# Two chained blocks on one core: the opening operands in three groups, the second expert block requested in the routing phase, and down weights as one run per partition

## What is computed

```python
silu_c = jax.nn.silu(c)
sh1, sc1, gt1, sh2, sc2, gt2 = jnp.split((silu_c @ ada_w[layer] + ada_b[layer])[:, None, :], 6, axis=-1)
...
hid = jnp.sin(freq * (feats @ w1 + b1))
hid = jnp.sin(freq * (hid @ w2 + b2))
filt = hid @ w3
filt = filt * jnp.exp(-t[:, None] * deltas[None, :])
filt = filt / jnp.sum(jnp.abs(filt), axis=0, keepdims=True)
...
def expert_block(args):          # once per block of rows of one expert
    xblk, e = args
    return (jax.nn.silu(xblk @ w1[e]) * (xblk @ w3[e])) @ w2[e]
```

## Time and profile before

| | us |
|---|---|
| median of 3 runs | 4396.33 (4392.52 to 4397.52) |
| the profiled execution | 4396.28 |
| its span, first to last instruction | 4394.5 |
| mean granted TensorE clock | 0.958 |

### The profile page before, as it was taken

One profiled execution on the slowest core, in us unless ns is written; L12 is line 12 of the kernel. 1 busy time (PEld: TensorE's weight loads), 2 busy tenths in 40 slices (PEclk: granted clock), 3 DMA queues, 4 the chain that ended last, 5 costly groups with the idle time before them and its releaser, 6 DMA issues. The chain is left out here.

```text
span 4394.5 us, 95415 instructions
## 1 busy us (share of the span) xinstructions
PE 3982.7 (91%) x41485; PEld 2613.4 (59%) x41485; DVE 1482.2 (34%) x2542; ACT 1014.7 (23%) x2416; POOL 605.7 (14%) x732
## 2 busy tenths in 40 slices
PE   7798999998999969999978999989999989997995
PEld 2343446885444458888854444469888944445774
DVE  2555412133121320000042666655566532222003
ACT  2200110032010112222243442034444311112333
POOL 1030000001100000000010001334454311000112
PEclk8899999999999979999989999989999999997997
DMA  6362302003112079999971001100000031124998
GB/s 214 117 200 81 129 24 72 29 10 66 38 37 93 34 286 390 391 396 398 396 250 28 10 2 43 43 2 4 4 3 4 4 97 43 58 84 183 392 388 316
DMA packets 233424, 588.67 MB, mean 134 GB/s; under 512 B 36456, under 2 KB 140807, under 8 KB 213224
## 3 DMA queue, kind: packets, MB, share of 16 engines
q1 hardware_dynamic: 192447, 462.92, 28.9%
q0 software_dynamic: 19120, 73.68, 4.9%
q10 hardware_dynamic: 21626, 48.70, 3.2%
HBM read 514.20 MB, written 71.05 MB: 133 GB/s over the span
## 5 line engine op out<-in xcount | busy, mean ns | idle before, releaser
L1650 PE MATMUL experts_bank<-experts_uT,ex_wu 128*64 128x96 f32 x9216 | 391.5, 247 | 27.0 <-PE experts_bank L1636 21.3
L1650 PEld LDWEIGHTS experts_bank<-experts_uT,ex_wu 128*64 128x64 f32 x9216 | 385.1, 138 | 43.7 <-issue 43.7
L1723 DVE TENSOR_TENSOR experts_hT<-experts_si,experts_bank 128x384 f32<-128x384 f32 (+1 forms) x68 | 31.3, 460 | 723.1 <-PE experts_bank L1650 723.1
L192 PE MATMUL vgproj_bank<-vg_w,mix_hT 128*128 128x256 f32 x1024 | 225.7, 383 | 11.1 <-DVEq L201 7.7
L192 PEld LDWEIGHTS vgproj_bank<-vg_w,mix_hT 128*128 128x128 f32 x1024 | 195.7, 192 | 41.5 <-DVEq L201 8.5
L1650 PE MATMUL experts_bank<-experts_uT,b2z_hT 128*64 128x96 f32 x4096 | 177.7, 248 | 25.3 <-DMA b2z_hT<-in_w 12.7
L1650 PEld LDWEIGHTS experts_bank<-experts_uT,b2z_hT 128*64 128x64 f32 x4096 | 172.2, 138 | 40.0 <-issue 40.0
L1636 PE MATMUL experts_bank<-mixed_T,experts_hT 128*32 128x256 f32 (+1 forms) x2592 | 193.9, 451 | 0.0
L2247 POOL TENSOR_TENSOR b2z_hT<-b2z_hT,rwkv_level 128x256 f32<-128x256 f32 x192 | 153.8, 833 | 159.3 <-DVE b2z_hT L2600 159.2
L2616 DVE TENSOR_TENSOR rc_xy<-rc_xy,rc_bank 128x256 f32<-128x256 f32 x288 | 120.6, 420 | 122.3 <-PE rc_bank L2261 116.4
L1636 PEld LDWEIGHTS experts_bank<-mixed_T,experts_hT 128*32 128x32 f32 x2592 | 110.4, 110 | 69.6
(11 more groups left out here) (576 smaller groups left out, 7195.4 us busy)
## 6 DMA issues: line engine op xcount, KB each, us to landing
ex_wu<-in_expert_w SPq DMA_DIRECT2D x72, 2048.0 KB
mixed_T<-in_expert_w SPq DMA_DIRECT2D x36, 2048.0 KB, 23.0
b2z_hT<-in_w SPq DMA_DIRECT2D x64, 1024.0 KB
b2z_Z<-in_w SPq DMA_DIRECT2D x32, 1024.0 KB, 12.4
keep_rows<-mix_hyT ACTq DMA_DIRECT2D x27, 768.0 KB
keep_rows<-experts_yo ACTq DMA_DIRECT2D x68, 288.0 KB
mix_hT<-in_ada_w POOLq DMA_DIRECT2D x8, 2048.0 KB, 9.9
merge_w<-in_w_in SPq DMA_DIRECT2D x32, 512.0 KB, 6.1
```

Source lines behind the costliest of these rows:

```text
L192: last = pe.matmul(bk[t][:, 0:width], xT[:, k, t * P:(t + 1) * P], wt[:, s, k, :], start=(k == 0), stop=(k == KT - 1))
L1650: last = pe.matmul(bk[2 + j][c:c + 64, h * BT:(h + 1) * BT], wu[:, s, j, k, h * P + c:h * P + c + 64], uT[:, s, k, :], start=(k == 0), sto ...
```

## The change

Three edits. (1) The opening: ACT's nine operands are split into `fed` (features, first layer), `layered` (the three vectors and the second layer) and `spread` (third layer, `negt`, `delta`), and each user waits for its own group. The first 16 of the 23 vectors stay on SP's queue, the other 7 are requested by ACT between `layered` and `spread`. POOL waits for `layered` before its first request of `ada_w`. (2) The routing phase requests the weights of block zero and of block one, and the loop of the expert phase starts with block two; its last load outside the loop is gone. (3) `w2` is laid out by `experts_to_runs` too, so that partition p holds the hidden rows 4p to 4p+3 (2p and 2p+1 in the second mixture). For the hidden values to come out in that order, the up products take as stationary operand every fourth (every second) column of `wu`, which is a step of 16 (8) bytes.

```diff
--- before.py
+++ after.py
@@ -154,10 +154,6 @@
 def rows_to_tiles(ap):
 
     return ap.rearrange("l (k p) n -> p (l k) n", p=P)
-
-
-def experts_to_tiles(ap):
-    return ap.rearrange("l e (k p) n -> p (l e) k n", p=P)
 
 
 def experts_to_runs(ap):
@@ -612,20 +608,25 @@
         wfull = m.sems(*[f"wfull{n}" for n in range(RING)])
         loaded, zeroed, turned, cols_ok, silu_ok, ada_mm, ada_out, ada_cols = m.sems(
             "loaded", "zeroed", "turned", "cols_ok", "silu_ok", "ada_mm", "ada_out", "ada_cols")
-        come, browed, lin, chain, sine, mm, decs, fls, abss, sums = m.sems(
-            "come", "browed", "lin", "chain", "sine", "mm", "decs", "fls", "abss", "sums")
+        fed, layered, spread, browed, lin, chain, sine, mm, decs, fls, abss, sums = m.sems(
+            "fed", "layered", "spread", "browed", "lin", "chain", "sine", "mm", "decs", "fls", "abss", "sums")
         vectors = [v for v in VECS if v]
         ada_w = rows_to_tiles(I["ada_w"])
         b = m.block()
+        SPLIT = 16
+
+        def row_of(name, n):
+
+            g, r = divmod(PLACES[name][0], P)
+            return rows[r:r + n, g, :], flat(I[name]).rearrange("(n p) -> n p", p=P)
 
         @b.sync
         def _(sp):
             sp.dma_start(K.ident[:, :], I["k_eye"]).then_inc(loaded, 16)
             sp.dma_start(adasum[:, :], I["k_adasum"]).then_inc(loaded, 16)
             sp.wait_ge(zeroed, 1)
-            for name, n in vectors:
-                g, r = divmod(PLACES[name][0], P)
-                sp.dma_start(rows[r:r + n, g, :], flat(I[name]).rearrange("(n p) -> n p", p=P)).then_inc(loaded, 16)
+            for name, n in vectors[:SPLIT]:
+                sp.dma_start(*row_of(name, n)).then_inc(loaded, 16)
 
         @b.gpsimd
         def _(gp):
@@ -636,6 +637,7 @@
             gp.memset(one2[:, :], 0.0).then_inc(zeroed, 1)
             gp.wait_ge(zeroed, 5)
             gp.memset(one2[:, 0:2], 1.0).then_inc(zeroed, 1)
+            gp.wait_ge(layered, 64)
             for n in range(ADA):
                 if n >= RING:
                     gp.wait_ge(ada_mm, ada_item(n - RING) + 1)
@@ -684,13 +686,14 @@
                 if t >= 1:
                     norm_sum(t - 1)
 
-            pe.wait_ge(come, 16 * 9)
+            pe.wait_ge(fed, 32)
             for x in range(2):
                 pe.matmul(fm[x][0:64, :], w1[:, :], feats[:, x * HALF:(x + 1) * HALF], start=True, stop=True).then_inc(lin, 1)
             pe.wait_ge(loaded, 16 * (2 + len(vectors)))
             for g in range(VGROUPS):
                 pe.transpose(cb[:, g * P:(g + 1) * P], rows[:, g, :], K.ident[:, :]).then_inc(turned, 1)
             pe.wait_ge(sine, 1)
+            pe.wait_ge(layered, 64)
             for x in range(2):
                 pe.matmul(fm[x][0:64, :], w2[:, :], hid[:, x * HALF:(x + 1) * HALF], start=True, stop=True).then_inc(lin, 1)
             pe.wait_ge(silu_ok, 2)
@@ -701,6 +704,7 @@
                 ada_rows(n)
                 ada_turn(n - 1)
             pe.wait_ge(sine, 2)
+            pe.wait_ge(spread, 48)
             for t in range(NT):
                 filt(t)
                 if t in (1, 3, 4, 6):
@@ -715,11 +719,16 @@
 
         @b.scalar
         def _(act):
-            loads = [(feats[:, :], I["k_feats"]), (w1[:, :], I["hy_ffn_w1"][0]), (vecs[:, 0:1], I["hy_ffn_b1"].rearrange("a p -> p a")),
-                     (vecs[:, 1:2], I["hy_ffn_freq"].rearrange("a p -> p a")), (vecs[:, 2:3], I["hy_ffn_b2"].rearrange("a p -> p a")),
-                     (w2[:, :], I["hy_ffn_w2"][0]), (w3[:, :], I["hy_ffn_w3"][0]), (negt[:, :], I["k_negt"]), (delta[:, :], I["k_delta"])]
-            for dst, src in loads:
-                act.dma_start(dst, src).then_inc(come, 16)
+            for to, what in ((feats[:, :], I["k_feats"]), (w1[:, :], I["hy_ffn_w1"][0])):
+                act.dma_start(to, what).then_inc(fed, 16)
+            for to, what in ((vecs[:, 0:1], I["hy_ffn_b1"].rearrange("a p -> p a")), (vecs[:, 1:2], I["hy_ffn_freq"].rearrange("a p -> p a")),
+                             (vecs[:, 2:3], I["hy_ffn_b2"].rearrange("a p -> p a")), (w2[:, :], I["hy_ffn_w2"][0])):
+                act.dma_start(to, what).then_inc(layered, 16)
+            act.wait_ge(zeroed, 1)
+            for name, n in vectors[SPLIT:]:
+                act.dma_start(*row_of(name, n)).then_inc(loaded, 16)
+            for to, what in ((w3[:, :], I["hy_ffn_w3"][0]), (negt[:, :], I["k_negt"]), (delta[:, :], I["k_delta"])):
+                act.dma_start(to, what).then_inc(spread, 16)
             act.dma_start(brow[:, :], I["ada_b"]).then_inc(browed, 16)
 
             def ada_evac(n):
@@ -750,6 +759,7 @@
             act.wait_ge(chain, 12)
             act.activation(hid[:, :], arg[:, :], ACT.Sin).then_inc(sine, 1)
             ada_evac(3)
+            act.wait_ge(spread, 48)
             for t in range(NT):
                 if t >= 2:
                     act.wait_ge(fls, 2 * (t - 1))
@@ -767,7 +777,7 @@
         @b.vector
         def _(dve):
             then = Chain(dve, chain)
-            dve.wait_ge(come, 16 * 9)
+            dve.wait_ge(layered, 64)
             for n in range(2):
                 dve.wait_ge(lin, 2 * n + 2)
                 if n:
@@ -1346,10 +1356,11 @@
                 sp.wait_ge(yok, t + 1)
                 sp.dma_start(y_dram[tok(t), :], ys[:, t % SLOTS, :]).then_inc(ysaved[t % SLOTS], 16)
             sp.wait_ge(chosen, 1)
-            e = sp.value_load(T.be[0:1, 0:1], min_val=0, max_val=NE - 1)
-            for j, wj in enumerate((w1, w3)):
-                sp.dma_start(T.wu[:, 0, j, :, :], wj[:, bass.ds(e, 1), :, :].rearrange("p a k n -> p (a k) n")).then_inc(T.wufull[0], 16)
-            sp.dma_start(T.wd[:, 0, :, :], w2[:, bass.ds(e, 1), :, :].rearrange("p a k n -> p (a k) n")).then_inc(T.wdfull[0], 16)
+            for n in range(2):
+                e = sp.value_load(T.be[0:1, n:n + 1], min_val=0, max_val=NE - 1)
+                for j, wj in enumerate((w1, w3)):
+                    sp.dma_start(T.wu[:, n, j, :, :], wj[:, bass.ds(e, 1), :, :].rearrange("p a k n -> p (a k) n")).then_inc(T.wufull[n], 16)
+                sp.dma_start(T.wd[:, n, :, :], w2[:, bass.ds(e, 1), :, :].rearrange("p a k n -> p (a k) n")).then_inc(T.wdfull[n], 16)
 
         @b.gpsimd
         def _(gp):
@@ -1599,11 +1610,9 @@
 
             n1 = sp.value_load(T.nb[0:1, 1:2], min_val=1, max_val=MAXB // 2 - 1)
             with sp.Fori(0, n1) as i:
-                for s in (1, 0):
-                    e = sp.value_load(T.be[0:1, bass.ds(i * 2 + (2 - s), 1)], min_val=0, max_val=NE - 1)
-                    load(s, e, i * 2 + (3 - s))
-            e = sp.value_load(T.be[0:1, bass.ds(n1 * 2 + 1, 1)], min_val=0, max_val=NE - 1)
-            load(1, e, n1 * 2 + 2)
+                for s in range(2):
+                    e = sp.value_load(T.be[0:1, bass.ds(i * 2 + (2 + s), 1)], min_val=0, max_val=NE - 1)
+                    load(s, e, i * 2 + (3 + s))
             for dst, src, sem in ahead:
                 sp.dma_start(dst, src).then_inc(sem, 16)
 
@@ -1647,7 +1656,7 @@
                         for h in range(HT):
                             for k in range(KT):
                                 for c in (0, 64):
-                                    last = pe.matmul(bk[2 + j][c:c + 64, h * BT:(h + 1) * BT], wu[:, s, j, k, h * P + c:h * P + c + 64],
+                                    last = pe.matmul(bk[2 + j][c:c + 64, h * BT:(h + 1) * BT], wu[:, s, j, k, :].rearrange("p (q h) -> p h q", h=HT)[:, h, c:c + 64],
                                                      uT[:, s, k, :], start=(k == 0), stop=(k == KT - 1))
                         last.then_inc(up, 1)
                     pe.wait_ge(xfull[1 - s], i * 16 + (16 + 16 * s))
@@ -3216,7 +3225,7 @@
 
 
     rgw, rgb, rew, reb, w1, w3, w2 = names
-    ws = (experts_to_runs(I[w1]), experts_to_runs(I[w3]), experts_to_tiles(I[w2]))
+    ws = tuple(experts_to_runs(I[n]) for n in (w1, w3, w2))
     with Mem(nc, f"ex{tag}") as mx:
         T.wu = mx.sb("wu", [P, 2, 2, KT, hidden]) if wu is None else wu.rearrange("p k (s n) -> p (k s) n", n=hidden).rearrange("p (s j k) n -> p s j k n", s=2, j=2)
         T.be = mx.sb("be", [1, MAXB], I32)
```

## The result

The changed kernel takes 4556.54 us (median of 4 runs, 4551.66 to 4559.55) where the kernel before takes 4396.93 (4392.52 to 4399.69): a ratio of 1.0366, 95% interval 1.0353 to 1.0379. Forecast were 4384.7 us, in a range of 4371 to 4400. The profiled execution took 4557.07 us (span 4555.3), 160.8 more than the span before.

A forecast was written before the change was run, and what follows sets the result against it. TensorE, busy 91% of the span, was taken as the bound, so savings count only where it waits. 4396.3 - 13.1 (opening) + 2.5 + 2.0 (entries) - 3.0 (stage-two waits) = 4384.7 us, range 4371 to 4400.

The forecast's parts named there:

- rival 2: Up products, first stage alone: strided halves take turns at the load at the 16-byte step; +110 us, 4495 us, chance 0.07.
- The opening: Start of the program: the first product no longer waits for all nine operands; 13.1 us gained, range -15 to -6.
- the 1.5 us forecast for the fourth item: Opening, fourth `ada_w` load: lands at about 32.5 us, wanted at 31, so TensorE waits 1.5 rather than 1.2 us.
- the -15 of the range: Start of the program: the largest gain allowed for the opening, in a range of -15 to -6 us, clock uncertain.
- The entries: Start of both expert stages: block zero's gather competes with more queued weights; +2.5 us in the first, +2.0 in the second.
- +9: Both stage entries together: upper bound, if the gather takes 9.3 us in stage two and 2 us more in stage one.
- The waits at the end of stage two: Up products of stage two: a lead of a whole block removes the excess wait for weights; -3.0 us, other bound 0.
- w2 by runs, the SP loop: Expert stages: longer w2 runs help only where DMA is awaited, and the reordered loop issues the same loads; 0 us.
- The columns: Up products: the strided rate is the rate of plain fp32 loads, so strided columns cost 0; bounds 0 and 24 ns a pair.
- The rule quoted beside it: Strided loads: the skill's 16-byte cachelines need two hits for full rate, so 8-byte steps are free and 16-byte ones not.
- Rival 1: Up products, both stages: strided halves take turns at the load, 24 ns a pair; +159 us, 4544 us, chance 0.10.
- 0 to 24 ns: Up products: bounds on the extra load time of a pair of strided halves, the upper if they take turns.

The follow-up runs named there:

- the kernel without part 3: The changed kernel with w2 by tiles of 4 KB rows and contiguous columns, keeping the new opening and block one's early weight requests: 4389.71 us, ratio 0.9988.
- e11: Opening in three groups only, with w1 and w3 laid out by pairs of rows, so transposes load columns 8 bytes apart: 4395.80 us, ratio 0.9995.
- part 1 alone: The kernel before with only the opening in three groups of operands: 4384.48 us, ratio 0.9971.
- e6: The kernel before, stage one's column groups read at 4, 8, 12 and 16 bytes, transposes contiguous; only durations count: 81, 82.5, 87, 119 ns a pair.
- part 2 alone: The kernel before with only block one's weights requested in the routing phase and the reordered SP loop: 4402.47 us, ratio 1.0017.
- part 3 alone: The kernel before with only w2 by runs and the strided columns: 4565.75 us, ratio 1.0391.

## Why the columns cost

**An 8-byte step in both stages.** The changed kernel with w2 in two runs of two rows for each partition of stage one, so that the columns of an up product lie 8 bytes apart:

```
-    wu[:, s, j, k, :].rearrange("p (q h) -> p h q", h=HT)[:, h, c:c + 64]
+    wu[:, s, j, k, :].rearrange("p (a q h) -> p a h q", a=HT // 2, h=2)[:, h // 2, h % 2, c:c + 64]
-    w2: "l e (p k) n -> p (l e) k n"
+    w2: "l e (a p h) n -> p (l e) a (h n)", h=2
```

> The changed kernel with another order of the hidden units in stage one: a partition gets w2 as two runs of two rows (8 KB each), so the stationary operand of the up products is read with 8 bytes between columns in both stages; stage two is as in the changed kernel. Theory: only steps of 16 bytes and more load slower; the up products of stage one are back at 10.8 us a block (85 ns a pair of halves), and the time is that of the kernel without part 3, 4390 us (ratio 0.9988). Rival: any step costs once 36 blocks of four column groups are read, and stage two is spared only because it waits for its weights anyway: between 4390 and 4556.

Measured: 4389.52, 0.9989 (0.9980 to 0.9997), what parts 1 and 2 alone give:

```profile
L1659 PE MATMUL experts_bank<-experts_uT,ex_wu 128*64 128x96 f32 x9216 | 390.2, 247 | 26.2 <-PE experts_bank L1645 22.0 <-ACT experts_uT L1687 2.9 <-issue 1.3
```

Of the two steps only that of 16 bytes costs. This is rival 2 of the prediction.

**Steps of 4 to 16 bytes side by side.** This run and the three like it below are one execution each; only durations inside it are read. In stage one each of the four column groups has its own step and its own line:

```
+    wu[:, s, j, k, 0:64]     wu[:, s, j, k, 448:512]      (L1656, L1657)
+    wu[:, s, j, k, 0:128:2]  wu[:, s, j, k, 384:512:2]    (L1659, L1660)
+    wu[:, s, j, k, 0:192:3]  wu[:, s, j, k, 320:512:3]    (L1662, L1663)
+    wu[:, s, j, k, 0:256:4]  wu[:, s, j, k, 256:512:4]    (L1665, L1666)
     transposes: xg[:, slot, k * P:(k + 1) * P]
```

> The kernel before; in stage one the four column groups of an up product are read with 4, 8, 12 and 16 bytes between columns, each on a source line of its own, and the transposes of the gathered rows read contiguous columns instead of 32 bytes apart. It computes with the wrong columns, so only durations count. Theory (a load runs at full rate only when two of its columns lie in one 16-byte piece of memory; this is what the Trainium skill says in SBUF - State Buffer, in its note on cachelines): a pair of halves takes 85 ns at 4 and 8 bytes; at 12 bytes half of the columns have a neighbour in their piece, so 0.75 of 122 = 92 ns; at 16 bytes 122 ns. The eight transposes, 0.96 us before, fall to 0.6 or less. Rivals: the cost grows with the distance crossed (85, 97, 110, 122); or it belongs to the pair of halves alone and a single load has one rate whatever its step: then the transposes stay at 0.96.

The first load of each group of 16 pairs, from the timeline of PEld:

```profile
1910.93 0.13 PEld L1656 LDWEIGHTS experts_bank<-experts_uT,ex_wu 128*64 128x64 f32 x1 [0.86 <-issue]
...
1912.22 0.14 PEld L1659 LDWEIGHTS experts_bank<-experts_uT,ex_wu 128*64 128x64 f32 x1
...
1913.54 0.16 PEld L1662 LDWEIGHTS experts_bank<-experts_uT,ex_wu 128*64 128x64 f32 x1
...
1914.93 0.20 PEld L1665 LDWEIGHTS experts_bank<-experts_uT,ex_wu 128*64 128x64 f32 x1
...
1916.83 0.15 PEld L1656 LDWEIGHTS experts_bank<-experts_uT,ex_wu 128*64 128x64 f32 x1
```

From start to start, over 16: 81, 82.5, 87 and 119 ns a pair for 4, 8, 12 and 16 bytes, where 85, 85, 92 and 122 were expected; the rival of a cost that grows with the distance (97 at 8 bytes) is out. The transposes, now contiguous, take 0.70 us of loads for eight, not the 0.6 or less expected, but less than the 0.96 of before, and 62.9 us in all instead of 79.8:

```profile
1904.35 0.70 PEld L1631 LDWEIGHTS experts_bank<-all_ident,ex_xg 96*128 96x128 f32 x8
...
L1631 PEld LDWEIGHTS experts_bank<-all_ident,ex_xg 96*128 96x128 f32 x560 | 49.9, 143 | 24.7 <-issue 17.5
```

So a strided load is slower there too (204 ns against 143, the same instruction at another step), which the prediction had explained away.

**Larger steps, and one half strided alone.** Column groups: first half 4 bytes and second 16 (L1656, L1657), then both 32, both 20, both 24.

> The kernel before; in stage one the column groups are read with these bytes between columns, each on a line of its own: first half 4 and second half 16; both 32; both 20; both 24. It computes with the wrong columns, so only durations count. Theory (full rate needs two columns in one 16-byte piece, and the loads of the two halves follow one another): 32, 20 and 24 bytes all cost what 16 did, 122 ns a pair; the mixed pair takes 61 ns for the strided half and at most 32 for the contiguous one, 85 to 93. Rival 1: halves conflict only when both are strided: 85 mixed. Rival 2: the cost grows with distance or comes from powers of two: 32 bytes far above 122, or 20 and 24 below it.

```profile
1898.31 0.13 PEld L1656 LDWEIGHTS experts_bank<-experts_uT,ex_wu 128*64 128x64 f32 x1 [1.38 <-issue]
1898.32 0.19 PEld L1657 LDWEIGHTS experts_bank<-experts_uT,ex_wu 128*64 128x64 f32 x1
...
1900.22 0.22 PEld L1660 LDWEIGHTS experts_bank<-experts_uT,ex_wu 128*64 128x64 f32 x1
...
1902.18 0.21 PEld L1663 LDWEIGHTS experts_bank<-experts_uT,ex_wu 128*64 128x64 f32 x1
...
1904.01 0.21 PEld L1666 LDWEIGHTS experts_bank<-experts_uT,ex_wu 128*64 128x64 f32 x1
...
1905.87 0.22 PEld L1657 LDWEIGHTS experts_bank<-experts_uT,ex_wu 128*64 128x64 f32 x1
```

The second halves (L1657, L1660, L1663, L1666) advance every 119 ns at 16 bytes, 122 at 32, 114 at 20 and 116 at 24: from 16 bytes on, the distance changes little, and powers of two nothing. But the mixed pair was expected at 85 to 93 ns, and it runs at 119, no faster than with both halves strided. That is no sum of two loads. The theory that the halves' loads follow one another fell here, and so did rival 1, by which halves conflict only when both are strided.

**Loads of one half, and of all columns.** Stage one again: one half behind the other with 4 bytes (L1656, L1658), the same with 16 (L1660, L1662), 128 columns with 4 (L1664), 128 with 16 (L1666).

> The kernel before; in stage one the column groups are read so: loads of one half only, one behind the other, 4 bytes between columns; the same with 16 bytes; loads of all 128 columns with 4 bytes; the same with 16. It computes with the wrong columns, so only durations count. The mixed pairs of the run before showed the strided half moving on every 119 ns whether the other half was strided or not. So theory: a load reads strided columns at a rate of its own, the halves don't share it, and one strided half alone needs 119 ns, as a strided load of 128 columns needs about 110 to 120; contiguous, both are paced by the matmul of 96 columns. Rival (the halves take turns at one reader): a strided half alone needs only 60 ns and shows no cost.

```profile
1900.35 1.18 PEld L1656 LDWEIGHTS experts_bank<-experts_uT,ex_wu 128*64 128x64 f32 x14 [1.33 <-issue]
...
1902.66 1.42 PEld L1660 LDWEIGHTS experts_bank<-experts_uT,ex_wu 128*64 128x64 f32 x11
...
1906.05 1.86 PEld L1664 LDWEIGHTS experts_bank<-experts_uT,ex_wu 128*128 128x128 f32 x16
1907.83 3.81 PEld L1666 LDWEIGHTS experts_bank<-experts_uT,ex_wu 128*128 128x128 f32 x16
1911.73 1.18 PEld L1656 LDWEIGHTS experts_bank<-experts_uT,ex_wu 128*64 128x64 f32 x14
```

A half at 4 bytes: (1.18 - 0.14) / 13 = 80 ns from load to load; at 16 bytes (1.42 - 0.22) / 10 = 120. All 128 columns: (1907.83 - 1906.05) / 16 = 111 ns contiguous, (1911.73 - 1907.83) / 16 = 244 at 16 bytes. So with 16 bytes a plain load takes 1.9 ns a column (120 / 64, 244 / 128), with 4 bytes 0.87 or less (111 / 128). A strided half costs 120 ns alone and 119 with a strided neighbour: the halves load side by side. The up product then goes by the slower of two things, the pace of the pairs of matmuls (some 82 ns) and the load of one half: 64 * 0.87 = 56 ns stays below it, 64 * 1.9 = 122 doesn't. I had expected 110 to 120 for the strided load of 128 columns; 244 is twice that, because I had taken the transposes' rate again. The rival of one reader, 60 ns for a strided half alone, fell.

**Two kinds of load.** For plain loads the time from start to start is read, for transposes the duration of one load and the time of a group of eight. The eight transposes with 4, 8, ... 32 bytes, each on its own line (L1630 to L1637); up products of 128 columns with 4, 8 and 12 bytes (L1662, L1664, L1666), then halves with 8 (L1668).

> The kernel before; the eight transposes of the gathered rows read columns 4, 8, 12, 16, 20, 24, 28 and 32 bytes apart, each on its own line, and in stage one the up products load all 128 columns with 4, 8 and 12 bytes between them, and the two halves one behind the other with 8. It computes with the wrong columns, so only durations count. Theory (two kinds of load): a transpose has two rates, 143 ns contiguous and 204 to 215 at any step, 8 bytes included; a plain load of 128 columns needs 111 ns at 4 and at 8 bytes, some more at 12 (0.75 of the 244 measured at 16, 183), and the halves at 8 bytes 65 each as at 4. Rival: one rule for both, so that a transpose at 8 bytes takes 143 and what slowed e11 was something else; or plain loads of 128 columns are slower at 8 bytes too, and the halves hid it.

```profile
1903.60 1.86 PEld L1662 LDWEIGHTS experts_bank<-experts_uT,ex_wu 128*128 128x128 f32 x16
1905.38 1.96 PEld L1664 LDWEIGHTS experts_bank<-experts_uT,ex_wu 128*128 128x128 f32 x16
1907.27 2.85 PEld L1666 LDWEIGHTS experts_bank<-experts_uT,ex_wu 128*128 128x128 f32 x16
1910.22 1.19 PEld L1668 LDWEIGHTS experts_bank<-experts_uT,ex_wu 128*64 128x64 f32 x14
...
L1637 PEld LDWEIGHTS experts_bank<-all_ident,ex_xg 96*128 96x128 f32 x70 | 14.8, 211 | 0.0
L1631 PEld LDWEIGHTS experts_bank<-all_ident,ex_xg 96*128 96x128 f32 x70 | 13.9, 198 | 0.0
L1630 PEld LDWEIGHTS experts_bank<-all_ident,ex_xg 96*128 96x128 f32 x70 | 9.8, 140 | 26.7 <-issue 17.8 <-DMA ex_xg<-keep_normed,experts_now 1.1
```

Plain loads of 128 columns, from start to start: 111 ns at 4 bytes, 118 at 8 (111 expected), 184 at 12 (183 were expected of columns that share a 16-byte piece half of the time), and 244 at 16 in the run above. The halves at 8 bytes, expected at 65 ns each, go at (1.19 - 0.14) / 13 = 81, as they do at 4. Transposes, duration of one load: 140 ns at 4 bytes, 198 already at 8, 211 at 32, up to 231 between (204 to 215 were expected). Here each has neighbours of other steps. In the kernel with the rows in pairs, below, all eight have 8 bytes:

```profile
1893.80 1.03 PEld L1645 LDWEIGHTS experts_bank<-all_ident,ex_xg 96*128 96x128 f32 x8
```

So eight loads of transposes take 0.70 us at 4 bytes, 1.03 at 8 and 0.96 at 32. A plain load becomes much slower only behind 8 bytes, a transpose's load is slower at 8 already. A row of one kind can't price the other. Why the two differ stays open.

The Trainium skill, "SBUF — State Buffer", section "Door 1: The DMA port swizzle", in its note on cachelines, says that two accesses must fall into one 16-byte line for the full rate. The plain loads agree, with 118 ns at 8 bytes and 244 at 16. The transposes don't, with 198 at 8. The note also gives the stride that is free as "4 fp32"; taken as 16 bytes between columns, that does not hold here. The same skill, "TensorE: Matmul & The Clock Gate", section "LDWEIGHTS (loading the stationary operand)", gives columns / 1.2 ns for a load, 107 ns for 128; the contiguous plain load agrees with its 111 from start to start. The contiguous transposes follow one another faster, (0.70 - 0.14) / 7 = 80 ns.

## Can it be made faster

**Down weights behind the gather.** Part 1, and SP requests block zero's w2 only after `sp.wait_ge(xfull[0], 16)` at the start of the expert stage.

> The opening in three groups, part 2 and 3 undone, and block zero's down weights (2 MB, 1 MB in stage two) requested only when the gather of block zero has landed, at the start of the stage. If the entry is set by how many bytes are queued ahead of the gather (9.1 us from its request to the transposes with 6.3 MB ahead, 13.5 with 12.6), then with 4.2 MB ahead, which have passed by the time of the request, it should land in about 3 us: 4.5 less in stage one, 1 to 1.5 less in stage two, 4378.5 us against 4384 for the opening alone (ratio 0.9958 against 0.9971). Rival: the landing has a floor of its own of about 4 us, or the down weights are now late for the first down product: within 2 us of the opening alone.

Measured: 4382.02, 0.9962 (0.9949 to 0.9975), not to be told from part 1 alone (0.9960 to 0.9983). The first gather does land after 4.0 us (3 were expected, and 4 was the rival's floor), and its transposes start after 5.75 us instead of 9.07. It is given back behind: the idle time before the up products grows from 27.4 to 32.1 us in stage one and from 26.8 to 31.1 in stage two. In part 1's trace the two stages move 392 and 385 GB/s, in this one 393 and 379, all at a DMA share of 1.01 or 1.02: with the DMA engines busy all the time, what one transfer wins another loses.

**Rows in pairs.** Part 1, w1 and w3 as `"l e (c p h) n -> p (l e) c (h n)"` with h = 2, transposes with 8 bytes.

> The opening in three groups, parts 2 and 3 undone, and w1 and w3 laid out by pairs of rows (partition p holds rows 2p and 2p+1 of each 256), so that the transposes of the gathered rows load columns 8 bytes apart instead of 32. Theory: what e6 showed for contiguous columns, 0.25 us less for each group of eight transposes (1.13 to 0.88 us), 70 groups, all on TensorE's path: 17.5 us less than the opening alone, 4366.5 us (ratio 0.9931). Price: the transfers of w1 and w3 go in pieces of 4 KB and 2 KB rather than 16 and 8 KB. Rival: the shorter pieces slow the transfers, and stage two, which already waits for its weights some 16 times, waits longer: the gain is 10 us or less.

Measured: 4395.80, 0.9995 (0.9986 to 1.0004), 10.6 us more than part 1 alone. The transposes take 84.7 us instead of 79.7 (8 bytes gain them nothing, as the run above showed afterwards), and stage two, with pieces of 2 KB, waits 36.0 us instead of 26.8. With the late down weights added:

> The pairs of rows and the late down weights together on the opening in three groups. If the two are independent, their gains add: 4384 - 17.5 - 5.5 = 4361 us (ratio 0.9919). Rival: block zero's down weights, now among block one's shorter pieces, come late, and the sum falls short by 3 us or more.

Measured: 4396.42, 0.9990 (0.9981 to 0.9998). It is slower than part 1 alone (0.9971), and some 30 us short of the sum expected.

**Contiguous transposes in stage one.** Part 1, w1 and w3 of stage one by tiles.

> The opening in three groups, parts 2 and 3 undone, and in stage one w1 and w3 by tiles (a partition holds rows p, p + 128 and so on), so that the transposes there read contiguous columns; stage two as before. Theory: 35 groups of transposes at 0.25 us give 8.8 us, if the pieces of 2 KB keep the transfers at the 392 GB/s that stage one needs: 4384 - 8.8 = 4375 us (ratio 0.9951). Rival: stage one already moves 392 GB/s, its DMA engines busy all the time; shorter pieces move less, TensorE waits for weights, and nothing is left: 4384 or more.

```profile
L1664 PE MATMUL experts_bank<-experts_uT,ex_wu 128*64 128x96 f32 x9216 | 398.7, 250 | 46.2 <-DMA ex_wu<-in_expert_w 31.2 <-PE experts_bank L1650 11.6 <-ACT experts_uT L1692 3.0
...
L1645 PE MATMUL experts_bank<-all_ident,ex_xg 96*128 96x96 f32 x560 | 70.8, 270 | 17.6 <-issue 17.6
```

Measured: 4402.69, 1.0009 (1.0001 to 1.0018). The transposes give the 8.8 us expected (79.7 to 70.8). The pieces of 2 KB take them: 31.2 us of waits for weights, idle time 46.2 instead of 27.4 (+18.8), up products 398.7 instead of 391.4 (+7.3). 18.8 + 7.3 - 8.9 = 17.2, and the ratios say 0.38%, 16.7 us. Why the up products themselves slow down by 7.3 us is not shown.

**Conditioning weights sooner.** Part 1, and POOL waits for the first two operands (`gp.wait_ge(fed, 32)`) instead of the six.

> The opening in three groups, parts 2 and 3 undone, and the conditioning weights requested when the first two operands have landed instead of the first six, about 2 us sooner. Theory: the waits for them, 0.9 us at the third product and 0.4 to 1.2 at the fourth, shrink; the first one waits for the bias row, which then comes later among the larger loads. A gain of 1 us at most, 4383, no difference that can be told (ratio 0.9965 to 0.9975). Rival: the six small operands and the vectors, now among 6 MB of traffic, land late as before the change, and up to 10 us of the gain are gone (ratio 0.9990 or more).

Measured: 4379.90, 0.9956 (0.9943 to 0.9969). The vectors land later (L694's place at 14.65 us instead of 12.87 in part 1's trace), the third conditioning product has no wait, as in part 1's trace, the fourth one of 1.16 (0.38 there). It is faster than the kernel before and the changed one, as part 1 alone is. Between it and part 1 the intervals overlap, and nothing is claimed.

## Why the prediction was wrong, point by point

- **The opening: right, its agreement to 0.1 us partly luck.** 13.1 us forecast, 13.2 at its end in the pair of traces, 13.1 in the mean of eight, 12.7 in time (7.5 to 17.6). L691 starts at 4.13 (4.3), L698 at 15.25 (15 to 16), L656 at 19.54 (19 to 20). The vectors arrive at 13.3, just ahead of the sine. A wait of 0.62 us for the bias row `brow` was not foreseen; the one at the third item is 0.87 (0.3). The first DMA wait in the items comes at 28.49, and the 1.5 us forecast for the fourth item, at 31, aren't there: it starts at 35.06 without a wait. Before, it starts at 45.77, so the lead there is only 10.7: the granted clock is 0.65 and 0.50 from 28 to 36 us, in and behind the third item, which before ran at 1.00 and 0.94 (38 to 46 us). At the sixth item the lead is 15.1 (76.39 and 61.32), at the end 13.2. The forecast named the clock as its uncertainty, and here its turns nearly cancel. No run shows where the -15 of the range would come from: L691 starts 14.1 us earlier in the pair, 14.3 in part 1 alone.
- **The entries: right in kind, the first low in size.** +2.5 and +2.0 forecast; +4.6 and +1.8 in the pair, +4.8 and +2.0 in part 2 alone. The first gather lands after 11.8 us. The term was sized by a single gather of the loop (9.3), and that one was quick: the 35 gathers in the loop of the same trace, from 1580 to 2180 us, have a median of 11.2, which is near what was measured. +9 was the bound.
- **The waits at the end of stage two: wrong.** -3.0 forecast, on a "lead of a whole block". But the change moves only block one's first request. From then on a load is still requested when its buffer comes free, two blocks ahead, as before, and the transfers run at 387 GB/s before and 381 after with the DMA engines busy all the time (share 1.02 and 1.00), so that the stage's traffic sets these waits. 15.7 us of idle time are put down to weights after, 12.7 before. Three of the four profiles with part 2 have as much idle time in all before these up products as those without (25.2 to 26.3 against 24.0 to 26.8). The fourth, with only 4.4 us put down to weights, has 22.2, which is 3.1 less than before. So the size of the term was sensible, but part 2 doesn't reliably bring it, and why that one profile waits less is not shown.
- **w2 by runs, the SP loop: right as far as seen.** 0 forecast, 0 seen in stage one for the runs. The loop was not run apart from part 2, whose loss leaves 0.7 us for it.
- **The columns: wrong, and all of the miss.** The step that failed is "the strided rate is the rate that plain fp32 loads have". It set a strided load (L1631, 0.96 us for eight) beside a contiguous one (L662, 0.97) and took them as equal. They are equal by accident: the one is a transpose's, where the step costs (0.96 against 0.70), the other a plain product's, where 111 ns from start to start is the contiguous rate and 244 the strided one. The same row, 204 against 143 ns between two transposes, was like against like and said that a step costs; it was the better reading.
- **Rival 2: right in its place, 61 us short.** It had the first stage alone, which part 3 alone and the 8-byte step show. Its price, 24 ns a pair, came from the transpose's 109 ns. A plain strided load of a half takes 119 to 122, so 37 ns a pair more than 85 in the changed kernel (2 * 562.7 us / 9216 = 122), 36 * 128 * 37 = 170 us. Its evidence against (L1091 at 8 bytes as slow as L1631 at 32) was true, and true of transposes only. Its picture, halves that take turns, was wrong; it named the right stage because it went by the step. The rule quoted beside it was set aside on the row of L1091 too; for plain loads it holds (118 ns at 8 bytes, 244 at 16).
- **Rival 1: wrong.** Stage two's up products did not move, 178.4 against 177.7.
- **The chances.** 0.07 for the case that came, 0.17 for any cost of the columns. The bound "0 to 24 ns" was called a bound and rested on rows of another kind of load; the measured 37 lies outside.

With the measured terms the sum is 4396.3 - 13.1 + 4.6 + 1.8 + 171.2 = 4560.8 us; the runs lie at 4551.7 to 4559.6, just below.

## What to carry to other kernels

Price an access pattern only by rows of the same kind of instruction, and compare strided with contiguous within that kind; two durations that agree across kinds prove nothing. Before a layout is changed to lengthen DMA runs, look at which byte step it hands to TensorE: here 8 bytes were free and 16 bytes cost 44% of the up products, and an order of the units that keeps pairs together avoided it. Size a wait by the median of many such transfers, not by one row. Where the DMA engines were already busy all the time, as in both stages of the kernel before, an earlier or a later request only moved the wait to another transfer.

## What was not expected of the hardware

- A plain fp32 stationary operand of 128 columns loads every 111 ns (4 bytes between columns), 118 (8), 184 (12) and 244 (16). For halves of 64 columns at 16, 20, 24 and 32 bytes it is 119, 114, 116 and 122 ns.
- The two 64-column halves load side by side: one strided half costs 120 ns alone, 119 with a contiguous or a strided neighbour.
- One load of a transpose's stationary operand lasts 140 to 143 ns contiguous and 198 to 231 at any other step from 8 to 32 bytes; eight of them take 0.70 us contiguous, 0.96 at 32 bytes and 1.03 at 8. Which of these steps is the slowest isn't settled: 8 bytes took 198 ns on one line and 215 in the kernel with the rows in pairs.
- The first gather of the first stage (96 rows) lands after 4.0 to 4.1 us where 4.2 MB of weights were requested ahead of it, 7.3 to 7.9 with 6.3 MB, and 11.6 to 12.0 with 12.6 MB.
- Pieces of 2 KB instead of 16 KB in stage one: 382 GB/s at a busy share of 1.04, instead of 392 at 1.02. The idle time before the up products and the up products together grew by 26 us with it.
